# First layer norm by tile and halves, and loads reordered, at the start of a two-block transformer kernel

## The chip, the cores and the metric

The kernel runs on one core of a Trainium2 chip. The metric is device time in microseconds (us) of one execution. The kernel before was run three times.

## What is computed

The reference is a chain of transformer blocks on x of shape 1 x 256 x 1024 in float32: a block with two layers (mixer of latent attention, retention and block attention, then a dense feed-forward in the first and a mixture of experts in the second layer), then a second block with dilated attention, gating and cross attention. Only its first two steps matter here:

```
x = layer_norm(x, ln_emb_g, ln_emb_b)      # 256 rows, each over 1024 columns
h = x @ w_in[0]                            # 1024 -> 2656 columns
```

## The kernel before

The 256 rows of x are two tiles (t = 0, 1) of 128 partitions. Both x and every weight are split into a high part of type float32r (whi, xth) and the rest (wlo, xtl); a product is three matmuls, lines 577 to 579. All weights come as one stream of chunks through six raw buffers, loaded in order by SyncE (`load`, line 399; from the seventh chunk on a load waits for a low part to be done). For each chunk ScalarE makes the high part (`hi`, line 1514, busy line 1518) and VectorE the low part (`lo`, line 2009, busy line 2011); there are three places for split chunks, so the high part of chunk 3 waits until TensorE has released chunk 0. `advance(n)` makes the parts up to chunk n; LEAD is 2. The order of work on each engine is the order of the code; semaphores tie the engines together.

The input projection of a layer has six groups of columns. Group 0 (416 columns) uses chunks 0 and 1 (1664 numbers a partition), group 1 (512 columns) chunks 2 and 3 (2048 numbers a partition). Chunks 4 and 5 (1152 and 768 numbers) are for the latent projections. `in_part(g, j, t)` (line 1121) multiplies the j-th chunk of group g with tile t: 12 matmuls. If the stage is not in BY_TILE, group 0 runs chunk 0 for both tiles, then chunk 1 for both; if it is, tile 0 with both chunks, then tile 1, and the turns of tile 1 (`turn_half`) stand inside these parts.

The start, before the first mixer:
- SyncE loads both tiles of x, the scale row (rows0, into bc), the identity, the shift row (rows1), then chunks 0 to 5 (lines 404 to 420).
- GpSimd issues the columns (cols), then waits for the first normed tile and issues the constant table (cst, 2180 KB), the positions and, when both tiles are normed, the next two rows.
- VectorE waits for both tiles of x, takes mean and variance of tile 0 (`measure_first`, line 2078) and norms the two tiles in whole rows of 1024 (`norm_embedding`, line 2104; busy lines 2114 to 2119).
- ScalarE takes the second moments of tile 1 (`ln_roots`, line 1549).
- TensorE turns both tiles by 128 x 128 (`transpose_x`, line 606, busy line 611) into four banks, and ScalarE and VectorE copy and split them in four pieces (`split_x`, lines 1542 and 2032).
- Around that the engines make chunks 0 (before the split) and 1 (behind it). VectorE then waits for cols and the constant table (lines 2655 and 2656) before it goes on to chunk 2.

The helpers by tile are there already and are used by the later norms ln1_0, ln2_0 and ln1_1: `norm_by_halves` (line 2051), `split_half` (line 2044), `split_tile` (line 1560), `turn_half` (line 652), `ln_by_tile` (line 1583, whose second moments are lines 1592 to 1595).

Of the kernel before, what the change touches and what calls it, by code (L numbers as in the profile page):

```python
# [17 lines left out]
ALU = mybir.AluOpType  # L18
ACT = mybir.ActivationFunctionType
# [6 lines left out]
T = 2  # L26
S = T * P
D = 1024
# [4 lines left out]
LEAD = SPLIT - 1  # L33
# [55 lines left out]
B_TQ, B_S, B_TP, B_O = 7, 0, 1, 2  # L89


BY_TILE = ("ln1_0", "ln2_0", "ln1_1")
X_TURNS = ((2, 3), (6, 7))


# [71 lines left out]
def _by_layer(*parts, skip=()):  # L167
    return [(f"{n}{l}", c) for l in LAYERS for n, c in parts if f"{n}{l}" not in skip]
# [17 lines left out]
    "x": [("emb", T)] + _by_layer(("lat", T), ("mix", 5), ("ln1_", T), ("ln2_", T))  # L186
    + [("mix2", 2 * T)],

    "half": _by_layer(("ln1_", T), ("ln2_", T), skip=("ln2_1",)),

    "mv": [("emb", 1)] + _by_layer(("ln1_", 1), ("ln2_", 1), skip=("ln2_1",)) + [("ln2_1", T)],

# [63 lines left out]
def program(nc, stream, x_in, mem_in, pos_in, consts, route_in, cols_in, rows_in, ws_in, blank_in, out):  # L256
    with ExitStack() as ctx:
# [5 lines left out]
        def sem(name):  # L263
            if name not in sems:
                sems[name] = ctx.enter_context(nc.semaphore(name))
            return sems[name]

        def at(stage, kind, count):

            if stage == "f1" and kind in UNIT_KINDS:  # L270
                return sem(f"f1_{kind}"), count
            return sem(kind), count + before(stage, kind)
# [21 lines left out]
        x = sb("resid", [P, T, D])  # L294
        r = sb("r", [P, T, D])
# [101 lines left out]
        @block.sync  # L397
        def _(sp):
            def load(c):
                if not (isinstance(c.n, int) and c.n < RAW):  # L400
                    sp.wait_ge(lo_done, c.n - RAW + 1)
                sp.dma_start(raw[:, c.raw, 0:c.width], stream[c.n, :, 0:c.width]).then_inc(landed[c.raw], 16)

            for t in range(T):
                sp.dma_start(r[:, t, :], x_in[t * P:(t + 1) * P, :]).then_inc(sem(f"x_in{t}"), 16)
            sp.dma_start(bc[:, 0, :], rows_in[0, :].partition_broadcast(P)).then_inc(sem("rows0"), 16)
            sp.dma_start(ident, consts[:, CONST_AT["ident"][0]:CONST_AT["ident"][1]]).then_inc(sem("ident_in"), 16)
            sp.dma_start(bc[:, 1, :], rows_in[1, :].partition_broadcast(P)).then_inc(sem("rows1"), 16)
            n = 0
            while n < NCHUNK:  # L410
                if any(n == AT[f] for f in ("f0", "f1", "f2", "f3")):
                    name = next(f for f in ("f0", "f1", "f2", "f3") if n == AT[f])
                    loops = 3 * (U_MOE if name == "f1" else U_FF) // LB
                    with sp.Fori(0, loops) as it:
                        for j in range(LB):
                            load(Chunk(n + j, it))
                    n += loops * LB
                else:
                    load(Chunk(n))
                    n += 1  # L420
            for t in range(T):
                sp.wait_ge(sem("final"), t + 1)
                sp.dma_start(out[t * P:(t + 1) * P, :], r[:, t, :]).then_inc(sem("stored"), 16)
            sp.wait_ge(sem("stored"), 16 * T)
# [3 lines left out]
        def _(pool):  # L428
# [6 lines left out]
                    sem(f"rows{n}"), 16)  # L435

            pool.dma_start(cols[:, :], cols_in).then_inc(sem("cols_in"), 16)
            pool.wait_ge(*at("emb", "x", 1))
            pool.dma_start(cst[:, 0:CONST_AT["ident"][0]], consts[:, 0:CONST_AT["ident"][0]]).then_inc(sem("const_in"), 16)
            pool.dma_start(posi[:, :], pos_in).then_inc(sem("pos_in"), 16)  # L440
            chained = [0]
# [132 lines left out]
        def _(pe):  # L574
# [31 lines left out]
            def transpose_x(stage, src, kn=KD, banks=(0, 1, 2, 3), ready=None):  # L606

                for t in range(T):
                    pe.wait_ge(*(ready(t) if ready else at(stage, "x", t + 1)))
                    for k in range(kn):  # L610
                        m = pe.transpose(ps[banks[k // 2]][:, (k % 2) * S + t * P:(k % 2) * S + (t + 1) * P],
                                         src[:, t, k * P:(k + 1) * P], ident)
                        if t == T - 1 and (k % 2 == 1 or k == kn - 1):
                            m.then_inc(sem("tr"), 1)
# [727 lines left out]
                        m.then_inc(used if (l, t, n) == (0, 1, 1) else sem("pj"), 1)  # L1342

            pe.wait_ge(sem("ident_in"), 16)
            transpose_x("emb", x)
            xt_stage = "emb"
            for l in range(DEPTH):
                mixer(l, xt_stage)
# [155 lines left out]
        def _(act):  # L1504
# [3 lines left out]
            def link(ins):  # L1508

                chained[0] += 1  # L1510
                ins.then_inc(sem("act_chain"), 1)
                act.wait_ge(sem("act_chain"), chained[0])
# [7 lines left out]
            def advance(upto):  # L1520

                while cursor[0] <= min(upto, NCHUNK - 1):
                    hi(Chunk(cursor[0]))
                    cursor[0] += 1
# [21 lines left out]
                        act.activation(dst[:, k, :], ps[banks[b]][:, (k % 2) * S:(k % 2 + 1) * S], ACT.Copy,  # L1546
                                       scale=cols[:, gain + k:gain + k + 1]).then_inc(sem("xh"), 1)

            def ln_roots(stage, ready):


                act.wait_ge(*ready)
                link(act.activation(x[:, 1, :], r[:, 1, :], ACT.Copy, accum_out=ss[:, 0:1]))
                link(act.activation(ss[:, 1:2], ss[:, 0:1], ACT.Copy, scale=-1.0 / D))
                act.wait_ge(*at(stage, "mv", 1))
                act.activation(sd[:, 0:1], mv[:, 0, 1:2], ACT.Sqrt, bias=eps[:, 0:1]).then_inc(sem("sd"), 1)
                link(act.activation(x[:, 1, :], r[:, 1, :], ACT.Square, bias=ss[:, 1:2], accum_out=ss[:, 2:3]))
                act.activation(sd[:, 1:2], ss[:, 2:3], ACT.Sqrt, bias=eps[:, 0:1], scale=1.0 / D).then_inc(sem("sd"), 1)

            def split_tile(stage, t):  # L1560

                for b in range(2):
# [4 lines left out]
            def last_norm():  # L1567
# [3 lines left out]
                for t in range(T):  # L1571
# [4 lines left out]
                    for k in range(KD):  # L1576
                        act.wait_ge(*at("n1", "tr", 4 * t + k % 4 + 1))
                        if k >= 4:
                            act.wait_ge(*at("n1", "xt", KD * t + k - 3))
                        act.activation(xth[:, k, t * P:(t + 1) * P],  # L1580
                                       ps[TURN_BANKS[k % 4]][:, (k // 4) * S + t * P:(k // 4) * S + (t + 1) * P], ACT.Copy, scale=cols[:, COLS["ffn1"] + k:COLS["ffn1"] + k + 1]).then_inc(sem("xh"), 1)

            def ln_by_tile(stage, ready, upto=0):


                act.activation(sd[:, 3:4], eps[:, 0:1], ACT.Sqrt)
                act.wait_ge(*at(stage, "mv", 1))
                act.activation(sd[:, 0:1], mv[:, 0, 1:2], ACT.Sqrt, bias=eps[:, 0:1]).then_inc(sem("sd"), 1)
                advance(upto)
                split_tile(stage, 0)  # L1590
                act.wait_ge(*ready)
                link(act.activation(x[:, 1, :], r[:, 1, :], ACT.Copy, accum_out=ss[:, 0:1]))
                link(act.activation(ss[:, 1:2], ss[:, 0:1], ACT.Copy, scale=-1.0 / D))
                link(act.activation(x[:, 1, :], r[:, 1, :], ACT.Square, bias=ss[:, 1:2], accum_out=ss[:, 2:3]))
                act.activation(sd[:, 1:2], ss[:, 2:3], ACT.Sqrt, bias=eps[:, 0:1], scale=1.0 / D).then_inc(sem("sd"), 1)
                split_tile(stage, 1)

            def rms_roots(stage, tile_ready, junk, src):
# [273 lines left out]

            act.wait_ge(sem("eps_set"), 2)
            act.activation(sd[:, 3:4], eps[:, 0:1], ACT.Sqrt)
            ln_roots("emb", (sem("x_in1"), 16))
            advance(0)
            split_x("emb")
            advance(LEAD - 1)
            act.wait_ge(sem("cols_in"), 16)
            for l in range(DEPTH):  # L1880
                mixer(l)
# [117 lines left out]
        def _(dve):  # L1999
# [3 lines left out]
            def link(ins):  # L2003

                chained[0] += 1
                ins.then_inc(sem("dve_chain"), 1)
                dve.wait_ge(sem("dve_chain"), chained[0])
# [6 lines left out]
            def advance(upto):  # L2014

                while cursor[0] <= min(upto, NCHUNK - 1):
                    lo(Chunk(cursor[0]))
                    cursor[0] += 1
# [84 lines left out]

            def norm_embedding():

                for t in range(T):
                    dve.wait_ge(sem(f"x_in{t}"), 16)
                measure_first("emb", lambda n: None)
                dve.wait_ge(sem("rows0"), 16)
                for t in range(T):  # L2110
                    mean, sign = (mv[:, 0, 0:1], ALU.subtract) if t == 0 else (ss[:, 1:2], ALU.add)
                    if t == 1:
                        dve.wait_ge(*at("emb", "sd", T))
                    link(dve.scalar_tensor_tensor(out=r[:, t, :], in0=r[:, t, :], scalar=mean, in1=bc[:, 0, :],
                                                  op0=sign, op1=ALU.mult))
                    dve.wait_ge(*at("emb", "sd", t + 1))
                    link(dve.reciprocal(rstd[:, t:t + 1], sd[:, t:t + 1]))
                    dve.wait_ge(sem("rows1"), 16)
                    dve.scalar_tensor_tensor(out=x[:, t, :], in0=r[:, t, :], scalar=rstd[:, t:t + 1], in1=bc[:, 1, :],
                                             op0=ALU.mult, op1=ALU.add).then_inc(sem("x"), 1)  # L2120

            def half_sum(stage, t, n):

# [525 lines left out]
            for slot in range(2):  # L2649
                dve.memset(lone_keys[slot][HD * (1 - slot):HD * (2 - slot)], 0.0).then_inc(sem("blank_keys"), 1)  # L2650
            norm_embedding()
            advance(0)
            split_x("emb")
            advance(LEAD - 1)
            dve.wait_ge(sem("cols_in"), 16)
            dve.wait_ge(sem("const_in"), 16)
            for l in range(DEPTH):
# [374 lines left out]
```

## Time and profile before

| | us |
|---|---|
| median of 3 runs | 2038.57 |
| lowest and highest | 2038.34, 2038.59 |
| the profiled execution | 2039.05 |
| its span, first to last instruction | 2037.2 |

The page of the profile gives the busy time of each engine (PE is TensorE, PEld its weight loads, DVE VectorE, ACT ScalarE, POOL GpSimd, SP SyncE), the chain of work that ended last and the costliest groups of instructions. DVE is busy for 74% of the span, ACT for 61%. The timeline lists instructions in order of time: start, duration, engine, line, operation, output <- input, count, and in brackets the idle time of the engine before it and what ended it. Some rows merge several like instructions. Times count from the start of the span.

### The profile page before, as it was taken

The page shows a single profiled execution, that of the slowest core. Times are in us where ns is not written, and L with a number is a line of the kernel's source. Part 1 is how long each engine was busy: PE and PEld are TensorE (multiplying, and loading weights), DVE is VectorE, ACT ScalarE, POOL GpSimd, SP SyncE. Part 2 cuts the span into 40 slices and gives each one's busy share as a digit, 9 for nine tenths or more (in the row PEclk, how much of TensorE's full clock was granted, in tenths as well). Part 3 has the DMA queues.
Part 4 walks back from the last instruction along what each step waited for, and adds up shares of the span by engine and source line. Part 5 has one row for each costly group of instructions (what it writes and reads, how often), then busy time and mean ns, then how long its engine had stood idle before and what let it go on. Part 6 is the DMA issues. An engine that isn't in the chain of part 4 may idle for free.

```text
span 2037.2 us, 26427 instructions
## 1 busy us (share of the span) xinstructions
PE 1993.5 (98%) x9638; PEld 1668.3 (82%) x9638; DVE 1512.2 (74%) x1543; ACT 1244.7 (61%) x1324; POOL 103.6 (5%) x102
## 2 busy tenths in 40 slices
PE   7999999999999999999999999999899999999998
PEld 6978887889888888888888888887688889798886
DVE  6675546676988998898999889899864456655554
ACT  5555444555777777777777777776644455444443
POOL 0011000001000000000000000023000003000000
PEclk9999999999999999999999999999999999999999
DMA  8347654344999999999999999999755554444550
GB/s 330 121 149 293 220 186 154 137 181 174 420 385 383 378 377 369 389 374 381 378 380 384 378 381 377 367 399 372 279 216 185 185 176 165 145 146 176 187 190 33
DMA packets 79658, 555.06 MB, mean 272 GB/s; under 512 B 8976, under 2 KB 9104, under 8 KB 17632
## 3 DMA queue, kind: packets, MB, share of 16 engines
q1 hardware_dynamic: 73728, 522.98, 67.7%
q0 software_dynamic: 5840, 30.85, 4.0%
q8 instruction: 61, 1.00, 0.2%
q14 instruction: 29, 0.24, 0.0%
HBM read 544.88 MB, written 12.58 MB: 274 GB/s over the span
## 4 chain that ended last, share of the span: by engine, by line
PE 92%; DVE 5%; ACT 1%; issue 1%; DMA 0%; POOL 0%; SPq 0%; DVEq 0%; ACTq 0%
PE ps L577 29%; PE ps L579 28%; PE ps L578 28%; DVE wlo L2011 2%; PE ps L895 1%; PE ps L788 1%; ACT whi L1518 1%; PE ps L1217 0%; PE ps L1193 0%; PE ps L1224 0%; PE ps L1093 0%; PE ps L1073 0%; DMA bc<-in_rows 0%; PE ps L1241 0%; PE ps L1240 0%
## 5 line engine op out<-in xcount | busy, mean ns | idle before, releaser
L2011 DVE TENSOR_TENSOR wlo<-raw,whi 128x2048 fp32r<-128x2048 f32 (+4 forms) x505 | 1145.2, 2271 | 288.6 <-ACT whi L1518 282.1
L1518 ACT ACTIVATE whi<-raw 128x2048 fp32r<-128x2048 f32 (+4 forms) x505 | 950.3, 1883 | 182.8 <-PE ps L579 173.6
L577 PE MATMUL ps<-whi,xth 128*128 128x512 f32 (+3 forms) x1856 | 737.5, 397 | 9.0 <-DVE wlo L2011 5.1
L579 PE MATMUL ps<-whi,xtl 128*128 128x512 f32 (+3 forms) x1856 | 716.4, 386 | 0.0
L578 PE MATMUL ps<-wlo,xth 128*128 128x512 f32 (+3 forms) x1856 | 714.7, 385 | 0.0
L577 PEld LDWEIGHTS ps<-whi,xth 128*128 128x128 f32 x1856 | 350.8, 189 | 77.0 <-DVE wlo L2011 9.9
L579 PEld LDWEIGHTS ps<-whi,xtl 128*128 128x128 f32 x1856 | 350.2, 189 | 69.0
L578 PEld LDWEIGHTS ps<-wlo,xth 128*128 128x128 f32 x1856 | 351.5, 189 | 61.6
L579 PE MATMUL ps<-whi,htl 128*128 128x512 f32 (+2 forms) x748 | 290.1, 388 | 0.0
L577 PE MATMUL ps<-whi,hth 128*128 128x512 f32 (+2 forms) x736 | 287.3, 390 | 2.0 <-DVE htl L2304 1.0
L578 PE MATMUL ps<-wlo,hth 128*128 128x512 f32 (+2 forms) x736 | 284.5, 387 | 0.0
L577 PEld LDWEIGHTS ps<-whi,hth 128*128 128x128 f32 x736 | 138.2, 188 | 31.7 <-issue 2.9
L579 PEld LDWEIGHTS ps<-whi,htl 128*128 128x128 f32 x748 | 140.4, 188 | 28.9
L578 PEld LDWEIGHTS ps<-wlo,hth 128*128 128x128 f32 x736 | 138.2, 188 | 26.9
L1680 ACT ACTIVATE prob<-ps 128x256 f32<-128x256 f32 x112 | 43.0, 384 | 90.0 <-PE ps L579 90.0
L1689 ACT ACTIVATE hth<-ps 128x256 fp32r<-128x256 f32 x112 | 43.1, 384 | 83.2 <-PE ps L895 83.2
L1640 ACT ACTIVATE hth<-ps 128x512 fp32r<-128x512 f32 x30 | 17.9, 598 | 90.9 <-PE ps L788 90.9
L1629 ACT ACTIVATE prob<-ps,rstd 128x256 f32<-128x256 f32 x44 | 18.4, 470 | 73.6 <-PE ps L579 73.6
L2186 DVE TENSOR_TENSOR htl<-ps,hth 128x512 fp32r<-128x512 f32 x30 | 20.7, 691 | 43.3 <-ACT hth L1640 43.3
L2172 DVE SCALAR_TENSOR_TENSOR probt<-prob,rstd,ps 128x256 f32<-128x256 f32 x44 | 19.2, 476 | 39.5 <-ACT prob L1629 39.5
L2304 DVE TENSOR_TENSOR htl<-ps,hth 128x256 fp32r<-128x256 f32 x112 | 46.7, 417 | 1.5 <-ACT hth L1689 1.5
L2288 DVE TENSOR_TENSOR probt<-prob,ps 128x256 f32<-128x256 f32 x112 | 46.3, 413 | 0.0
(394 smaller groups left out, 1294.1 us busy)
## 6 DMA issues: line engine op xcount, KB each, us to landing
raw<-in_stream SPq DMA_DIRECT2D x475, 1024.0 KB, 6.6
raw<-in_stream SPq DMA_DIRECT2D x16, 768.0 KB, 4.5
bc<-in_rows POOLq DMA_DIRECT2D x4, 1024.0 KB, 5.8
slot_rows<-in_blank POOLq DMA_DIRECT2D x7, 512.0 KB, 10.6
kc<-slot_rows POOLq DMA_DIRECT2D x7, 512.0 KB, 8.1
sum_rows<-r POOLq DMA_DIRECT2D x7, 512.0 KB, 5.9
raw<-in_stream SPq DMA_DIRECT2D x4, 832.0 KB, 6.4
raw<-in_stream SPq DMA_DIRECT2D x4, 640.0 KB, 3.8
```

Of the source, the lines that this page charges most:

```text
L577: pe.matmul(o, ah, bh, start=start, stop=False, skip_group_check=True)
L578: pe.matmul(o, ah, bl, start=False, stop=False, skip_group_check=True)
L579: return pe.matmul(o, al, bh, start=False, stop=stop, skip_group_check=True)
L788: m = pe.transpose(ps[2][:, k * S + t * P:k * S + (t + 1) * P], hs[:, t, k * P:(k + 1) * P], ident)
L895: m = pe.transpose(ps[1][:, k * P:(k + 1) * P], hs[:, 0, k * P:(k + 1) * P], ident)
L1518: act.activation(whi[:, c.split, 0:c.width], raw[:, c.raw, 0:c.width], ACT.Copy).then_inc(hi_done, 1)
L1680: act.activation(sg[:, 0, :], ps[0][:, 0:FU], ACT.Silu).then_inc(sem("e_sg"), 1)
L1689: act.activation(hth[:, 0:2, 0:P], ps[1][:, 0:2 * P].rearrange("p (k s) -> p k s", k=2), ACT.Copy).then_inc(sem("e_hh"), 1)
L2011: dve.tensor_tensor(wlo[:, c.split, 0:c.width], raw[:, c.raw, 0:c.width], f32(whi[:, c.split, 0:c.width]), ALU.subtract).then_inc(lo_done, 1)
L2186: dve.tensor_tensor(htl[:, 0:2, :], ps[2][:, :].rearrange("p (k s) -> p k s", k=2), f32(hth[:, 0:2, :]), ALU.subtract).then_inc(unit_sem(n ...
L2288: dve.tensor_tensor(hs[:, 0, :], sg[:, 0, :], ps[0][:, FU:2 * FU], ALU.mult).then_inc(sem("e_h"), 1)
L2304: dve.tensor_tensor(htl[:, 0:2, 0:P], ps[1][:, 0:2 * P].rearrange("p (k s) -> p k s", k=2), f32(hth[:, 0:2, 0:P]), ALU.subtract).then_inc( ...
```

## The change

The first norm becomes one of the stages by tile. The loads are issued in another order: tile 0 of x, rows0, identity, rows1, chunk 0, tile 1 of x, chunk 1 and so on. VectorE norms and splits in halves of the columns, with chunk 0 ahead of tile 0's splits and chunk 1 ahead of the norm of tile 1. ScalarE takes the second moments of tile 1 behind chunk 1. GpSimd issues the constant table when both halves of tile 0 are split (semaphore xt at 2), where it waited for the first normed tile. Group 0 of the first input projection runs tile 0 with both chunks, then tile 1. RAISED counts what each semaphore is raised by in each stage.

```
-BY_TILE = ("ln1_0", "ln2_0", "ln1_1")
+BY_TILE = ("emb", "ln1_0", "ln2_0", "ln1_1")
...
-    "half": _by_layer(("ln1_", T), ("ln2_", T), skip=("ln2_1",)),
+    "half": [("emb", T)] + _by_layer(("ln1_", T), ("ln2_", T), skip=("ln2_1",)),
...
-            for t in range(T):
+            def rows_of_x(t):
                 sp.dma_start(r[:, t, :], x_in[t * P:(t + 1) * P, :]).then_inc(sem(f"x_in{t}"), 16)
+
+            rows_of_x(0)
...
+                if n == 1:
+                    rows_of_x(1)
...
-            pool.wait_ge(*at("emb", "x", 1))
+            pool.wait_ge(*at("emb", "xt", 2))
             pool.dma_start(cst[:, 0:CONST_AT["ident"][0]], consts[:, 0:CONST_AT["ident"][0]]).then_inc(sem("const_in"), 16)
...
             pe.wait_ge(sem("ident_in"), 16)
-            transpose_x("emb", x)
...
+            def second_moments(stage, ready):
+
+                act.wait_ge(*ready)
+                link(act.activation(x[:, 1, :], r[:, 1, :], ACT.Copy, accum_out=ss[:, 0:1]))
+                link(act.activation(ss[:, 1:2], ss[:, 0:1], ACT.Copy, scale=-1.0 / D))
+                link(act.activation(x[:, 1, :], r[:, 1, :], ACT.Square, bias=ss[:, 1:2], accum_out=ss[:, 2:3]))
+                act.activation(sd[:, 1:2], ss[:, 2:3], ACT.Sqrt, bias=eps[:, 0:1], scale=1.0 / D).then_inc(sem("sd"), 1)
...
-            ln_roots("emb", (sem("x_in1"), 16))
+            act.wait_ge(*at("emb", "mv", 1))
+            act.activation(sd[:, 0:1], mv[:, 0, 1:2], ACT.Sqrt, bias=eps[:, 0:1]).then_inc(sem("sd"), 1)
             advance(0)
-            split_x("emb")
+            split_tile("emb", 0)
             advance(LEAD - 1)
+            second_moments("emb", (sem("x_in1"), 16))
+            split_tile("emb", 1)
...
             def norm_embedding():
 
-                for t in range(T):
-                    dve.wait_ge(sem(f"x_in{t}"), 16)
+                dve.wait_ge(sem("x_in0"), 16)
                 measure_first("emb", lambda n: None)
                 dve.wait_ge(sem("rows0"), 16)
...
+                dve.wait_ge(sem("rows1"), 16)
+                norm_by_halves("emb", 0, mv[:, 0, 0:1], ALU.subtract)
+                advance(0)
+                for b in range(2):
+                    split_half("emb", 0, b)
+                advance(LEAD - 1)
+                dve.wait_ge(sem("x_in1"), 16)
+                dve.wait_ge(*at("emb", "sd", T))
+                norm_by_halves("emb", 1, ss[:, 1:2], ALU.add)
+                for b in range(2):
+                    split_half("emb", 1, b)
...
             norm_embedding()
-            advance(0)
-            split_x("emb")
-            advance(LEAD - 1)
             dve.wait_ge(sem("cols_in"), 16)
             dve.wait_ge(sem("const_in"), 16)
```

## Rows read from the trace of the kernel before

**Rows 1.** The page: busy time of TensorE, and the chain that ended last.
```profile
PE 1993.5 (98%) x9638; PEld 1668.3 (82%) x9638; DVE 1512.2 (74%) x1543; ACT 1244.7 (61%) x1324; POOL 103.6 (5%) x102
...
PE 92%; DVE 5%; ACT 1%; issue 1%; DMA 0%; POOL 0%; SPq 0%; DVEq 0%; ACTq 0%
```

**Rows 2.** The timeline of all engines, 0 to 28.3 us.
```profile
0.74 0.87 SPq L405 DMA_DIRECT2D r<-in_x  x2
...
5.59 1.28 DVE L2082 BATCH_NORM_STATS2 bn<-r 128x6 f32<-128x512 f32 x2 [4.08 <-DMA r<-in_x]
...
11.43 0.54 POOL L439 DMA_DIRECT2D cst<-in_consts  x1 [9.35 <-DVE resid L2119]
...
11.72 1.59 ACT L1518 ACTIVATE whi<-raw 128x1664 fp32r<-128x1664 f32 x1 [2.75 <-DMA raw<-in_stream]
...
15.55 2.48 DVE L2032 TENSOR_TENSOR xtl<-ps,xth 128x512 fp32r<-128x512 f32 x4
...
16.38 0.69 PE L577 MATMUL ps<-whi,xth 128*128 128x416 f32 x1 [0.52 <-DVE xtl L2032]
...
16.54 3.41 ACT L1518 ACTIVATE whi<-raw 128x1664 fp32r<-128x1664 f32 x2
...
22.41 0.36 PE L579 MATMUL ps<-whi,xtl 128*128 128x416 f32 x1
...
23.75 4.67 DVE L2011 TENSOR_TENSOR wlo<-raw,whi 128x2048 fp32r<-128x2048 f32 x2 [3.68 <-DMA cst<-in_consts]
...
28.28 0.39 PE L577 MATMUL ps<-whi,xth 128*128 128x512 f32 x1
```

**Rows 3.** Issues and time to landing: tile 0, rows1, chunk 0, chunk 1, constants.
```profile
r<-in_x SPq DMA_DIRECT2D x1, 512.0 KB, 3.5
...
bc<-in_rows SPq DMA_DIRECT2D x1, 512.0 KB, 7.0
...
raw<-in_stream SPq DMA_DIRECT2D x1, 832.0 KB, 8.4
...
DMA to landing us min/median/max: 10.0/10.0/10.0
...
cst<-in_consts POOLq DMA_DIRECT2D x1, 2180.0 KB, 12.2
```

**Rows 4.** Queues in 14 to 15, 19 to 20, 22 to 23 us: packets, MB, share.
```profile
q1 hardware_dynamic: 60, 0.43, 103.0%
...
q0 software_dynamic: 17, 0.30, 69.8%
q1 hardware_dynamic: 17, 0.14, 33.0%
...
q0 software_dynamic: 40, 0.12, 31.0%
```

**Rows 5.** The timeline of a later norm by halves, 138 to 147 us.
```profile
138.50 0.75 DVE L2055 SCALAR_TENSOR_TENSOR r<-r,mv,bc 128x512 f32<-128x512 f32 x1
...
140.81 0.75 DVE L2061 SCALAR_TENSOR_TENSOR resid<-r,rstd,bc 128x512 f32<-128x512 f32 x1
...
141.49 0.69 DVE L2048 TENSOR_TENSOR xtl<-ps,xth 128x512 fp32r<-128x512 f32 x1
...
143.53 1.06 ACT L1592 ACTIVATE resid<-r 128x1024 f32<-128x1024 f32 x1 [0.62 <-DVE r L2125]
...
146.23 0.29 ACT L1595 ACTIVATE sd<-ss,eps 128x1 f32<-128x1 f32 x1
```

**Rows 6.** TensorE's idle before two matmuls, and clock of a stretch (after POOL's busy).
```profile
146.48 0.50 PE L577 MATMUL ps<-whi,xth 128*128 128x512 f32 x1 [1.15 <-DVE wlo L2011]
...
1461.93 1.15 PE L665 MATMUL ps<-cst,resid 128*128 128x128 f32 x8 [3.82 <-DVE resid L2216]
...
1459.00:1475.00 16.00, 12.49 (x55) 10.06 (x56) 14.00 (x28) 8.79 (x23) 0.62 (x1) 0.89 0.35 119
```

More of the change, by code:

```diff
@@ L1547, in split_x @@
                                        scale=cols[:, gain + k:gain + k + 1]).then_inc(sem("xh"), 1)
[L1549 to L1558, printed above, removed]
             def split_tile(stage, t):
@@ L1590, in ln_by_tile @@
                 split_tile(stage, 0)
[L1591 to L1595, printed above, removed]
+                second_moments(stage, ready)
                 split_tile(stage, 1)
@@ L2104, in norm_embedding @@
             def norm_embedding():
-                for t in range(T):
-                    dve.wait_ge(sem(f"x_in{t}"), 16)
+                dve.wait_ge(sem("x_in0"), 16)
                 measure_first("emb", lambda n: None)
                 dve.wait_ge(sem("rows0"), 16)
[L2110 to L2120, printed above, removed]
+                dve.wait_ge(sem("rows1"), 16)
[9 more added lines that the diff above has]
+                    split_half("emb", 1, b)
             def half_sum(stage, t, n):
```

## Prediction

> **What bounds the kernel now.** I read the page first. TensorE is busy 1993.5 of 2037.2 us, and the chain that ended last lies 92% on it [rows 1]. So a change at the start can only shift the whole run: what counts is when TensorE starts, and whether it then runs on. Next I read the timeline of the first 30 us [rows 2]. The reader is to see four points. The first projection matmul starts at 16.38 us, released by the last step of splitting the turned activations (DVE line 2032 from 15.55). Group 0 of the input projection (48 matmuls) then runs without a gap. Group 1 starts at 28.28 us, the landmark of my sum. Its first weight chunk, chunk 2, was ready well ahead: its low part was made from 23.75 us, in 2.3 us, so at about 26.0 us. The slack is 2.2 us. That low part did not start earlier because VectorE waits for the constant table (cst), although ScalarE had made the high part by 20.0 us [rows 2]. After 28.28 us the waits of TensorE up to 150 us are all on work that itself follows TensorE (the 1.15 us before 146.48 is the longest, [rows 6]), so I carry a shift of the start of group 1 one to one to the end.
>
> **Landings.** Tile 0 of x is issued at 0.74 us and lands 3.5 later, at 4.24; tile 1 lands at about 5.5, since VectorE, which waits for both, starts at 5.59 [rows 2, 3]. One tile of x costs the queue 1.25 us. The second row (rows1) lands at 2.61 + 7.0 = 9.6, chunk 0 at 3.26 + 8.4 = 11.7, chunk 1 at 3.8 + 10.0 = 13.8 [rows 3]. Tile 1 of x now goes behind chunk 0, so rows1 lands at 8.35 and chunk 0 at 10.45. Chunk 1 has the same bytes ahead of it as before: 13.8.
>
> **Tile 0 to the first matmul.** Statistics of tile 0 start at 4.3 instead of 5.59 and end at about 5.8; that gain is hidden, since the norm now waits for rows1, until 8.45. From the same helper at 138.50: start of the norm to its last half 140.81 + 0.75, so 3.06 us, with the first half out after 1.6 [rows 5]. Here the halves are out at 10.1 and 11.55, and TensorE turns them by 12.7. ScalarE makes the high part of chunk 0 from 10.5 to 12.1 (1.59, [rows 2]), then the high parts of the halves of tile 0 (0.60 each) until 13.3. VectorE makes the low part of chunk 0 from 12.2 to 14.0 and then two half splits of 0.69 us [rows 5], done at 14.7 and 15.3. The first matmul follows at 14.85: 1.5 us earlier than 16.38. Both the shorter queue (1.25) and the half splits (four pieces of 0.6 before, the first of which was enough for the first matmul) are in it.
>
> **Group 0.** Its first 17 matmuls took from 16.38 to 22.41, 0.35 us each, which for 416 columns is the 1.2 GHz level; the other 31 took until 28.28, 0.19 each, the 2.4 GHz level [rows 2]; what TensorE had done before the rise was turns from 11.27 and matmuls from 16.38. The granted clock of the trace reads 1.00 all through this start, so I go by spacing. With the start 1.5 us earlier I expect the rise somewhere from 18.8 to 22.2 us. Tile 0, first chunk: 12 x 0.345 = 4.1, until 19.0. Chunk 1 is ready: high part 13.9 to 15.5, low part until 17.4.
>
> Tile 1 is now inside. ScalarE starts its second moments only behind chunk 1, at 15.5; the same block took from 143.53 to 146.23 + 0.29, 3.0 us [rows 5], so the root is there at 18.5. VectorE waits for it, and behind that wait stand the norm and splits of tile 1 and the low part of chunk 2. The halves of tile 1 come at 20.2 and 21.6. VectorE can split the first half only behind the second norm half: 21.6 to 22.3 at the earliest. TensorE gets there from 20.1 (rise at 18.8) and waits twice, some 0.6 and 0.5 us; with the rise at 22.2 it waits hardly at all, but runs slowly. The second half is turned at 24.1 to 25.2 and its high part is made by 24.75 to 25.9. Group 0 ends at 27.85 to 28.95. The eight turns of tile 1, now within the group, are in this (0.11 to 0.23 us each). So the 1.5 us gained at the start have shrunk to 0.4 us or to a loss of 0.7.
>
> **Chunk 2, which group 1 needs.** Two things now push it back.
> First, ScalarE's order. Its high part used to follow chunk 1 directly (16.54, two pieces, [rows 2]). Now the second moments and both splits of tile 1 stand ahead of it: it runs from 24.75 to 26.65 (25.9 to 27.8 with the late rise). The low part takes 2.28 more: 28.95 at the earliest.
> Second, the constants. GpSimd issued them at 11.43, 0.3 us behind the first x tile, and they landed 12.2 us later, at 23.6, just ahead of the low part at 23.75 [rows 2, 3]. The new condition is the second half split of tile 0, at 15.3: issue at 15.6. Queued behind that wait on GpSimd are the position load and the next rows, both needed late. How long they take: q0 moved nothing of them until 15.0, 3.6 us after the issue; then it got 0.30 MB a us against 0.14 MB of the weight queue, both with 17 packets [rows 4], so the queues take turns by packet and the 17 KB rows of the constants win over the 8 KB rows of weights. Their 2.23 MB ended soon after 22.0 [rows 4], 7.2 us, and landed 1.4 us later. In the new place they start 3.6 us after 15.6, at 19.2, when the weight queue at 0.43 MB a us is in chunk 5, with some 0.25 MB left in rows of 3 KB. Beside those the constants get 17 of 20 parts, 0.37 MB a us, for 4 us, then 0.30 for their last 0.75 MB: 6.5 us, and 1.4 to the landing: 27.1. Bounds: 25.8 if nothing else moves, 27.8 if it takes 12.2 again. I take 27.1, since the packet turns are seen directly. The low part of chunk 2 then runs from 27.2 to 29.5.
>
> *A rule against a row.* The row gives 12.2 us from issue to landing for 2180 KB [rows 3]. The Trainium skill, DMA: Bandwidth & Descriptors, section Anatomy of one DMA, gives about 2.0 us plus the bytes at 436 GB/s, an estimate of 7.1 us here. By that the constants would land at 22.7, the ScalarE order alone would set chunk 2, and the sum below would be +0.7. The trace does not agree, since the transfer shares its engines; I use the row.
>
> **Sum.** Group 1 starts at 29.5 instead of 28.28: +1.2 us. TensorE waits some 1.6 us ahead of it. What comes next has slack: chunk 3, whose high part waits until chunk 0's place is free (the third part of group 0 instead of the second) and follows at 28.5, is ready at 31.8 and needed at 35.0; the latent norm was in time by 3.3 us before and moves by about 0.5. Nothing of the arithmetic is added or removed; splitting the norm of two tiles in halves costs VectorE 0.5 us, all under other work. The profiled execution took 2039.05 us (span 2037.2), 0.48 above the median of 2038.57. So 2040.25 for a profiled run, and 2038.57 + 1.2 = 2039.8 for the median.
>
> **Rivals.**
> *A, chunk 2 is late (forecast): 0.70.* +0.7 (constants early, ScalarE sets it) to +1.9 (constants at 27.8, or late rise): 2039.3 to 2040.5. For it: both causes stand by themselves in the order of the code.
> *B, chunk 2 is in time: 0.16.* Then group 0's end decides: -0.4 us, 2038.2; if tile 1 also never waits, the whole 1.5 passes, 2037.1. For it: the slack was 2.2 us, and landings near the start may be faster than I place them. Against: ScalarE would have to reach chunk 2 two us earlier.
> *C, the wait drops the clock: 0.14.* TensorE idle for 1.6 us could fall back to 1.2 GHz. Behind the 3.82 us wait at 1461.93 the granted clock of the stretch is 0.89 [rows 6]; behind the 1.15 us wait at 146.48 the first matmul took 0.50 and nothing slow followed. My wait is nearer to the second. Price: a slow stretch like 16.38 to 22.2, half of which is lost, some 2.7 us: 2042.5 with +1.2, and 2043.1 with the constants at 27.8. Only the latter is slower by over 0.2%; it decides from a constants' landing of about 27.5 on.
> That the change doesn't do what it says is no rival of its own: the order is written out in the code.
>
> **Numbers.** 2039.8. The range 2038.1 to 2041.3 holds A with some margin and most of B; outside are the full gain and most of C. A measurement of this kernel tells from no change about 0.2%, 4.1 us; nearly all cases lie within. Faster needs group 1 at 24.2 us, which 48 matmuls from 14.85 don't allow unless all run at 2.4 GHz: 0.01. Slower is the end of C, with a little for a later wait that I don't see: 0.05. Same: 0.94.
>
> **What would show it.** First matmul near 14.85; group 1 near 29.5, waiting for the low part of chunk 2 (line 2011); its high part after the splits of tile 1 on ScalarE, from 24.7 on; constants issued near 15.6 and landed near 27. I am wrong if group 1 starts before 28.3, if TensorE never waits on line 2011 near 28 us, or if matmuls of 512 columns, now 0.23 us apart, follow that wait at about twice the spacing.

## The result: slower by 0.13%, with the loss ahead of group 1

The changed kernel takes 2042.53 us (median of 22 runs, 2040.24 to 2045.46), the kernel before, run beside it, 2039.52 (22 runs, 2036.84 to 2042.19). The ratio is 1.0013, interval 1.0007 to 1.0019: by the ratio 2.7 us slower, between 1.4 and 3.9 (the medians stand 3.0 apart). Forecast was 1.2 us slower and 2039.8 us, range up to 2041.3. The three runs known before the change (2038.34 to 2038.59) did not show that the kernel before itself scatters over 5 us. The profiled execution took 2043.17 us, its span is 2041.4, 4.2 more than the span before.

The page of the changed kernel, busy times and the chain that ended last; the lines answer to [rows 1]:

```profile
PE 1991.0 (98%) x9638; PEld 1665.2 (82%) x9638; DVE 1513.7 (74%) x1547; ACT 1246.3 (61%) x1324; POOL 103.3 (5%) x102
...
PE 92%; DVE 5%; ACT 1%; DMA 1%; issue 1%; SPq 0%; POOL 0%; DVEq 0%; ACTq 0%
PE ps L581 28%; PE ps L583 28%; PE ps L582 28%; DVE wlo L2010 2%; PE ps L899 1%; ACT whi L1521 1%; PE ps L792 1%; DMA cst<-in_consts 1%; DMA raw<-in_stream 0%; PE ps L1197 0%; PE ps L1221 0%; PE ps L1228 0%; PE ps L1097 0%; PE ps L1077 0%; PE ps L1244 0%
```

The work is the same, but the constants' load now lies on the chain (DMA 1%, where it was 0%). The timeline of the changed kernel at the start, against [rows 2] (lines 1521, 2010 and 2047 are the high part, the low part and the half split; 581 to 583 are the three matmuls):

```profile
9.76 0.75 DVE L2054 SCALAR_TENSOR_TENSOR r<-r,mv,bc 128x512 f32<-128x512 f32 x1 [4.15 <-DMA bc<-in_rows]
...
11.78 1.59 ACT L1521 ACTIVATE whi<-raw 128x1664 fp32r<-128x1664 f32 x1 [5.84 <-DMA raw<-in_stream]
...
13.41 1.89 DVE L2010 TENSOR_TENSOR wlo<-raw,whi 128x1664 fp32r<-128x1664 f32 x1 [0.58 <-ACT whi L1521]
...
15.22 1.28 DVE L2047 TENSOR_TENSOR xtl<-ps,xth 128x512 fp32r<-128x512 f32 x2
...
16.05 0.69 PE L581 MATMUL ps<-whi,xth 128*128 128x416 f32 x1 [2.05 <-DVE xtl L2047]
...
16.81 0.55 POOL L443 DMA_DIRECT2D cst<-in_consts  x1 [14.72 <-DVE xtl L2047]
...
25.91 3.71 ACT L1521 ACTIVATE whi<-raw 128x2048 fp32r<-128x2048 f32 x2
...
26.05 0.69 DVE L2047 TENSOR_TENSOR xtl<-ps,xth 128x512 fp32r<-128x512 f32 x1 [2.56 <-ACT xth L1556]
...
29.08 4.50 DVE L2010 TENSOR_TENSOR wlo<-raw,whi 128x2048 fp32r<-128x2048 f32 x2 [2.34 <-DMA cst<-in_consts]
...
31.43 0.50 PE L581 MATMUL ps<-whi,xth 128*128 128x512 f32 x1 [2.10 <-DVE wlo L2010]
```

The first matmul starts at 16.05 instead of 16.38, but group 1 at 31.43 instead of 28.28: 3.15 us later, behind a wait of 2.10 us for the low part of chunk 2. VectorE was free for that part from 26.7 on and ScalarE had finished its half at 27.8; it waited for the constants until 29.08. Their issue and landing, with those of rows1 and chunk 0 (columns as in [rows 3]):

```profile
bc<-in_rows SPq DMA_DIRECT2D x1, 512.0 KB, 7.5
...
raw<-in_stream SPq DMA_DIRECT2D x1, 832.0 KB, 9.2
...
DMA to landing us min/median/max: 12.2/12.2/12.2
```

The last line is that of the constants alone (line 443). They took 12.2 us as before, but from 16.81.

### The profile page after: what moved, and what is told of

Its sections match the earlier page's. It is cut to its first block, busy times and chain, and to the rows that moved or that the text cites. A ratio compares the mean times of both kernels' runs of the same rounds, so it can differ in the third digit from the quotient of the medians.

```text
span 2041.4 us, 26426 instructions
## 1 busy us (share of the span) xinstructions
PE 1991.0 (98%) x9638; PEld 1665.2 (82%) x9638; DVE 1513.7 (74%) x1547; ACT 1246.3 (61%) x1324; POOL 103.3 (5%) x102
## 4 chain that ended last, share of the span: by engine, by line
PE 92%; DVE 5%; ACT 1%; DMA 1%; issue 1%; SPq 0%; POOL 0%; DVEq 0%; ACTq 0%
PE ps L581 28%; PE ps L583 28%; PE ps L582 28%; DVE wlo L2010 2%; PE ps L899 1%; ACT whi L1521 1%; PE ps L792 1%; DMA cst<-in_consts 1%; DMA raw<-in_stream 0%; PE ps L1197 0%; PE ps L1221 0%; PE ps L1228 0%; PE ps L1097 0%; PE ps L1077 0%; PE ps L1244 0%
## 5 line engine op out<-in xcount | busy, mean ns | idle before, releaser
L899 PEld LDWEIGHTS ps<-cst,probt 128*128 128x128 f32 x224 | 30.9, 139 | 20.3 <-DVE probt L2286 6.0
```

The source lines that it names most:

```text
L899: m = pe.transpose(ps[1][:, k * P:(k + 1) * P], hs[:, 0, k * P:(k + 1) * P], ident)
```

## The experiments

Two starting points were used: the changed kernel and the kernel before. The number to watch is the start of group 1, read from each timeline. "Ratio" is always to the kernel before, run beside it.

**Second and third profiles.** Unchanged kernels, four profiles.

> The kernel before, unchanged, for a second profile of its start. If the landings scatter from run to run by up to 1.5 us, the scale row lands between 8.2 and 9.1 and group 1 starts between 28.3 and 29.2. If they don't, both are as in the first profile within 0.2 us.

> The changed kernel, unchanged, for a second profile of its start. If its late rows (9.7 us) were one draw, the shift row lands near 8.4, the first matmul is near 14.8, the constants are issued near 15.5 and land near 27.6, and group 1 starts near 30.1. If it is how the new order always comes out, group 1 is again near 31.4.

> The kernel before, a third profile. Group 1 at 28.3 to 28.7, no wait for chunk 2. If the fall of the clock between 108 and 118 us, seen in both profiles so far, belongs to this order of work, it is there again; if it comes by chance, it may be missing.

> The changed kernel, a third profile. Group 1 at 30.5 to 31.5, behind a wait of about 2 us for chunk 2. Waits of 2.10 and 2.12 us left the clock up in the two profiles so far, while waits of 2.18, 2.95 and 4.20 us in other versions were followed by a stretch at 1.2 GHz. If that is by chance, it can follow here too, at some 1.6 us.

| kernel | chunk 0 landed, about | first matmul | constants issued | group 1 | span |
|---|---|---|---|---|---|
| before | 11.7 | 16.38 | 11.43 | 28.28 | 2037.2 |
| before, second | 12.6 | 17.31 | 12.35 | 28.64 | 2039.4 |
| before, third | 11.4 | 16.10 | 11.15 | 27.64 | 2038.2 |
| changed | 11.8 | 16.05 | 16.81 | 31.43 | 2041.4 |
| changed, second | 11.0 | 15.24 | 16.00 | 30.58 | 2040.5 |
| changed, third | 12.0 | 16.27 | 17.04 | 31.48 | 2042.5 |

The landings scatter, by 1.2 us among the three profiles of the kernel before and by 1.0 among those of the changed one, so the late rows of the first profile were partly a draw. The profiles come from several batches on different chips, and it can't be told how much of this is the chip; e7 and e8 below, which have the same loads up to there and ran in one batch, still differ by 0.7. What doesn't scatter much is the distance from the first matmul to group 1: 11.9, 11.3 and 11.5 us before, 15.4, 15.3 and 15.2 after. On the means, the first matmul comes 0.7 us earlier and group 1 3.0 us later (28.19 to 31.16). Between the two lie 1.7 us more for group 0, which now holds the turns and splits of tile 1 (13.3 us from its first matmul to its end, against 11.6), and 2.0 us of waiting for chunk 2: -0.7 + 1.7 + 2.0 = 3.0. The spans differ by 3.2 us on the means. The timed difference, 2.7, is the same within its interval. The third profile of the kernel before misses its expectation (27.64 against 28.3 to 28.7): the scatter is wider than two profiles had shown. The fall of the clock behind the 2 us wait, which was thought possible there, did not come in the third profile of the changed kernel either.

**e1: the constants early.** Changed kernel with

```diff
-            pool.wait_ge(*at("emb", "xt", 2))
+            pool.wait_ge(*at("emb", "x", 1))
```

> The changed kernel, but the constant table is issued when tile 0 is normed (about 13.1 us) and not when it is split (16.8). In the changed kernel group 1 starts at 31.43 us, waiting for the low part of chunk 2, for which the constants (landed 29.0) came last; its high part was done at 27.8. Theory (two causes, the constants first and ScalarE's order 1.2 us behind them): the constants land near 25.3, the low part runs from 27.9 to 30.15, group 1 starts at 30.2, and the time falls by 1.2 us against the changed kernel, still 1.9 above the kernel before. Rival (the constants alone): group 1 starts where group 0 ends, at 29.15, a fall of 2.3 us. Rival (load order alone): no fall.

**e2: ScalarE's half of chunk 2 early.** Changed kernel with

```diff
             second_moments("emb", (sem("x_in1"), 16))
+            advance(LEAD)
             split_tile("emb", 1)
```

> The changed kernel, but ScalarE makes the high part of chunk 2 ahead of the splits of tile 1 (in its idle time from 19.7 to 22.2 us) and not behind them. Theory (the constants come last): the high part is done by 21.6, and nothing else moves: group 1 at 31.4 us, time as the changed kernel within 0.3 us. Rival (ScalarE's order is what sets chunk 2): the low part starts at 26.8, group 1 at 29.15, a fall of 2.3 us.

**e3: both edits.**

> Both edits: constants issued when tile 0 is normed, and the high part of chunk 2 ahead of the splits of tile 1. Theory: chunk 2 is then bound by VectorE alone, low part from 26.8 to 29.05, group 1 at 29.15 us where group 0 ends: 2.3 us below the changed kernel, 0.9 above the kernel before. Rival (something else than chunk 2 holds group 1): it starts later than 29.5.

The low part of chunk 2 and the start of group 1, from the timelines of e1, e2 and e3 (two lines each, in this order):

```profile
27.20 4.49 DVE L2010 TENSOR_TENSOR wlo<-raw,whi 128x2048 fp32r<-128x2048 f32 x2 [1.21 <-ACT whi L1521]
...
29.55 0.50 PE L581 MATMUL ps<-whi,xth 128*128 128x512 f32 x1 [0.96 <-DVE wlo L2010]
```

```profile
26.58 4.49 DVE L2011 TENSOR_TENSOR wlo<-raw,whi 128x2048 fp32r<-128x2048 f32 x2 [0.72 <-DMA cst<-in_consts]
...
28.93 0.50 PE L581 MATMUL ps<-whi,xth 128*128 128x512 f32 x1 [0.48 <-DVE wlo L2011]
```

```profile
25.72 4.48 DVE L2011 TENSOR_TENSOR wlo<-raw,whi 128x2048 fp32r<-128x2048 f32 x2
...
28.23 0.40 PE L581 MATMUL ps<-whi,xth 128*128 128x512 f32 x1
```

The brackets name the cause, whatever the landings were. With early constants the low part waits 1.21 us for ScalarE; with early ScalarE it waits 0.72 for the constants; with both it waits for nothing and TensorE doesn't either. So both causes are real, the constants the later of the two. In all three the first matmul came at 14.5 to 14.9, and from there to group 1 it is 14.7, 14.4 and 13.4 us against 15.3 of the changed kernel. e2's 14.4 is smaller than the theory wanted (15.3, no fall), since its constants took only 11.2 us to land. e1's 14.7 is larger than it wanted (14.1), since group 0 itself took 13.8 us there: 16 of its matmuls ran at the 1.2 GHz level, against 12 to 14 in the changed kernel. The times say less: ratios 1.0016 (1.0007 to 1.0025), 1.0015 (1.0006 to 1.0024) and 1.0010 (1.0001 to 1.0019). They don't show what one edit alone is worth. They do show a gain of both together: e3 ran beside e1 and e2, and on the means of 11 runs each it is 1.4 and 1.8 us faster (95% intervals 0.3 to 2.5 and 0.6 to 3.0).

**e4: chunk 2 ahead of the wait for the constants.** Changed kernel with the edit of e2 and, on VectorE,

```diff
-                for b in range(2):
-                    split_half("emb", 1, b)
+                split_half("emb", 1, 0)
+                advance(LEAD)
+                split_half("emb", 1, 1)
```

> The changed kernel, but both parts of chunk 2 are made ahead of the wait for the constants: the high part between ScalarE's second moments and its splits of tile 1, the low part between the two half splits of tile 1 on VectorE. The constants stay late. Theory (chunk 2's readiness is all that holds group 1): TensorE doesn't wait at the start of group 1; it starts where group 0 ends, some 13.3 us behind the first matmul, so at about 28 us with the rows landed at 8.4 and 29.2 with the late landing of the changed kernel's profile. Rival (the constants matter elsewhere too, as for the latent norm): a wait turns up before 45 us.

```profile
22.54 2.28 DVE L2011 TENSOR_TENSOR wlo<-raw,whi 128x2048 fp32r<-128x2048 f32 x1
...
28.15 2.29 DVE L2011 TENSOR_TENSOR wlo<-raw,whi 128x2048 fp32r<-128x2048 f32 x1 [2.28 <-DMA cst<-in_consts]
...
28.30 0.39 PE L581 MATMUL ps<-whi,xth 128*128 128x512 f32 x1
```

Chunk 2's low part fits into VectorE's idle time inside tile 1, the constants still come at 28.1, now in front of chunk 3, and TensorE has no wait for it (its only waits from 20 to 45 us are two of 0.3 us for half splits). Ratio 1.0004 (0.9995 to 1.0013): no difference to the kernel before can be told any more. By the mean distance of each to the kernel before, e4 is 1.7 us faster than the changed kernel (0.5 to 2.8), so the readiness of chunk 2 made most of the loss of 2.7. The repair ends level and not ahead: the wait is gone, but group 0 by tile still takes 13.7 us here against 11.6 before, which uses up what the earlier first matmul (14.60) gains.

**e5: late constants alone.** Kernel before with

```diff
-            pool.wait_ge(*at("emb", "x", 1))
+            pool.wait_ge(*at("emb", "xt", 1))
```

> The kernel before with one edit: the constant table is issued when the first piece of x is split (about 16.4 us) and not when tile 0 is normed (11.4). Theory (a late constant table is enough by itself): it lands near 28.6, the low part of chunk 2 is made from 28.7 to 31.0, group 1 starts at 31.0 instead of 28.28: 2.7 us above the kernel before, nearly the whole loss of the changed kernel. Rival (the order by tile and the loads make the loss): less than 1 us above the kernel before.

```profile
30.28 4.49 DVE L2011 TENSOR_TENSOR wlo<-raw,whi 128x2048 fp32r<-128x2048 f32 x2 [9.40 <-DMA cst<-in_consts]
...
32.62 0.80 PE L577 MATMUL ps<-whi,xth 128*128 128x512 f32 x1 [4.20 <-DVE wlo L2011]
...
34.07 0.63 PE L577 MATMUL ps<-whi,xth 128*128 128x512 f32 x1
...
38.92 0.40 PE L577 MATMUL ps<-whi,xth 128*128 128x512 f32 x1
```

One moved wait on GpSimd, with nothing else changed, costs 6.1 us: ratio 1.0030 (1.0018 to 1.0043). It is more than the 2.7 expected, for two reasons in the rows. Group 1 starts at 32.62, 4.4 us behind the mean of the kernel before (first matmul 17.18, constants issued 17.35, 12.8 us to landing). And TensorE, idle for 4.20 us, goes on at 0.43 us a matmul instead of 0.23, the 1.2 GHz level, until about 38.5: some 2.8 us more on the way to the next norm. The granted clock of 28 to 38 us reads 0.69. That is rival C of the prediction, in another kernel.

**e6: the old order of loads.** Changed kernel, both tiles of x first.

> The changed kernel with the old order of loads (both tiles of x first). Theory (one tile of x costs the queue 1.25 us): the shift row lands near 9.6 and chunk 0 near 11.7, the first matmul is near 16.0 instead of the 14.8 seen in three of the four profiles with the new order, the constants are issued near 16.8, and group 1 starts near 31.2. Rival (the order of loads is worth nothing, the landings only scatter): first matmul at 14.5 to 15.

Chunk 0's high part starts at 11.60, the first matmul is at 15.87, group 1 at 31.48 behind a wait of 2.95 us, after which the clock falls (granted 0.83 from 28 to 38 us); ratio 1.0026 (1.0016 to 1.0036). In the seven profiles that keep the new order and the old rows, chunk 0's high part starts at 10.2 to 12.0, at 10.9 on the mean; in the five with the old order at 11.4 to 12.6, 12.0 on the mean. The order of loads is worth about 1.1 us there, against the 1.25 that the prediction took for one tile of x, but a single profile can't show it: the three of the kernel before and the three of the changed kernel differ by 0.3 only.

**e7, e8, e9, e10: the queue at the start.** e7 is the changed kernel with the two rows laid out 128 times in main memory. e8 adds the edits of e4. e9 adds to e8 the identity behind chunk 0 and the columns behind the constants. e10 is the kernel before with wide rows, the identity behind rows1 and the columns behind the constants. The line of e7's edit for the scale row (the shift row's load changes likewise; the new input is left out here):

```diff
-            sp.dma_start(bc[:, 0, :], rows_in[0, :].partition_broadcast(P)).then_inc(sem("rows0"), 16)
+            sp.dma_start(bc[:, 0, :], wide_in[0]).then_inc(sem("rows0"), 16)
```

> The changed kernel, but the scale and shift rows stand 128 times in main memory, laid out so ahead, and are loaded as plain 128 x 1024 blocks. Theory (the slow stretch of the queue, 0.22 to 0.36 MB a us instead of 0.43 between 4 and 9 us, comes from 128 reads of one row): the rate stays near 0.43, the shift row lands near 7.4 us, chunk 0 near 9.5, the first matmul near 13.8. Rival (the slow stretch comes from the small packets of the columns and the identity): landings as in the changed kernel, 8.2 to 9.7.

> Both of the last edits: chunk 2 made ahead of the constants, and the rows wide in main memory. Theory: first matmul near 13.8, group 1 near 27.0, 1.3 us ahead of the kernel before, so a time 1 to 1.5 us below it. Rival: no gain over the kernel before, since later falls of the clock set the time.

> The kernel with wide rows and chunk 2 made ahead of the constants, and besides the small-packet loads moved back: the identity behind chunk 0, the columns behind the constants. Theory (the rest of the slow stretch at 5 us, 0.21 to 0.24 MB a us with 102 to 112 packets under 2 KB, is the identity and the columns): the rate stays at 0.37 or more, the shift row lands near 7.5, the first matmul is near 13.8, group 1 near 26.8. Rival (the stretch is slow whatever stands in it): as without the move, 14.3 and 27.3. Time: 1 us below the kernel before by the theory, if the start of group 1 is all that counts.

> The kernel before with the loads alone improved: wide rows, the identity behind the shift row, the columns behind the constants. Theory: the scale row lands near 7.0 instead of 8.2 to 9.1, the first matmul near 15.3, group 1 near 27.2, time 1 us below the kernel before. Rival (VectorE's whole-row norm is the longer path, so the landings don't matter): first matmul within 0.3 us of 16.4.

What the DMA engines moved in one us: 5 to 6 us of e7, then 5 to 6 and 8 to 9 us of e9, then 5 to 6 and 7 to 8 us of the kernel before and 5 to 6 us of e10.

```profile
DMA packets 145, 0.21 MB, mean 213 GB/s; under 512 B 24, under 2 KB 102, under 8 KB 145
```

```profile
DMA packets 86, 0.34 MB, mean 344 GB/s; under 512 B 2, under 2 KB 2, under 8 KB 86
...
DMA packets 184, 0.30 MB, mean 302 GB/s; under 512 B 27, under 2 KB 140, under 8 KB 184
```

```profile
DMA packets 70, 0.23 MB, mean 226 GB/s; under 512 B 14, under 2 KB 14, under 8 KB 70
...
DMA packets 218, 0.39 MB, mean 385 GB/s; under 512 B 26, under 2 KB 138, under 8 KB 218
...
DMA packets 92, 0.36 MB, mean 360 GB/s; under 512 B 4, under 2 KB 4, under 8 KB 92
```

In e7 and e9 the slow microsecond goes where the small packets of the identity go. Wide rows brought the scale row from 6.3 to 5.6 us and left that microsecond in place. But the kernel before is slow (0.23 MB) in a microsecond with hardly a small packet, which wide rows bring to 0.36 (e10), and moves 0.39 MB beside 138 of them. So each theory had a part: the scale row, read 128 times, cost the queue time, and small packets did in some microseconds and not in others; what decides that stayed open. About the 7.4 us expected of e7 for the shift row (found 8.7) came only with the small loads away (e9: issued 1.7, 5.8 later). First matmul 14.99, 14.32 and 13.78 in e7, e8 and e9, where 13.8 was expected of all three; group 1 at 30.28, 27.34 and 27.20 (27.0 and 26.8 expected of e8 and e9). Yet the ratios are 1.0009 (1.0000 to 1.0018), 1.0004 (0.9995 to 1.0013) and 0.9997 (0.9988 to 1.0006). e9 starts group 1 a full us ahead of the kernel before, and no gain can be told. e10 repeated the mistake under study: ScalarE waits for the columns ahead of chunk 2.

```profile
24.43 3.71 ACT L1518 ACTIVATE whi<-raw 128x2048 fp32r<-128x2048 f32 x2 [6.62 <-DMA cols<-in_cols]
```

Its first matmul is at 16.04, group 1 at 28.83 behind a new wait of 1.75 us, ratio 1.0001 (0.9992 to 1.0010): the expectation of 27.2 failed on a wait that I had moved without asking what is queued behind it. The first matmul missed its 15.3 too. In the five profiles with whole-row norms it comes 8.06 to 8.07 us behind the start of the norm of tile 0, which waits for the scale row, and VectorE is the longer path; here that row landed at 7.9 and not at 7.0.

## Why the prediction was wrong in size

**What bounds the kernel:** the prediction was right that a shift at the start is carried to the end, but on the way it isn't carried one to one. On the means of three profiles, group 1 moved by 3.0 us, the first turn of the next norm by 1.5 (140.07 to 141.59), the first turn of the last of these norms by 3.0 (1462.0 to 1465.0), the span by 3.2. The granted clock explains the dip; 108 to 118 us of before and of the changed kernel, the last three columns being the clock, the share of the DMA engines and GB/s:

```profile
108.00:118.00 10.00, 8.64 (x42) 7.28 (x42) 8.91 (x25) 5.63 (x15) 2.17 (x2) 0.83 0.42 148
```

```profile
108.00:118.00 10.00, 8.64 (x61) 7.72 (x60) 9.72 (x23) 7.48 (x21) 2.17 (x2) 1.00 0.29 106
```

In all three profiles of the kernel before the clock falls there, in none of the changed kernel; from group 1 to the next norm it is 111.9 us with that fall and 110.4 without. It also falls there in e1, e8 and e10 and not in e2 to e7 and e9, so it isn't tied to either order of work. What sets it stayed open. The 1.5 us come back later, up to 1462 us: 1.0 on the means in waits of TensorE among the experts, and 0.5 by a single pause in the third profile of the changed kernel. Its waits from 480 to 1455 us, before and changed (total, times, longest):

```profile
PE ps L577 <- DVE wlo L2011: 1.8, 2, 0.9
PE ps L895 <- DVE probt L2288: 1.6, 1, 1.6
PE ps L577 <- DVE htl L2304: 1.0, 1, 1.0
```

```profile
PE ps L899 <- DVE probt L2286: 4.8, 3, 1.7
PE ps L581 <- DVE htl L2302: 1.0, 1, 1.0
```

4.4 us in each of the three profiles of before, 5.8, 5.5 and 5.0 in those of the changed kernel, 4.3 to 6.0 in the other versions. The pause, where the other five of these profiles have 3.82 us:

```profile
1466.71 1.97 PE L669 MATMUL ps<-cst,resid 128*128 128x128 f32 x8 [5.20 <-issue]
```

Nothing in the profile ended its last 1.4 us. I did not forecast either, and why the sums differ was not settled.

**The first matmul:** forecast 14.85, found 16.05, 15.24 and 16.27. The chain was right: with chunk 0's high part started at 11.78, 10.97 and 12.01, the matmul is 4.26 to 4.27 us behind it each time, and 4.35 was the sum. The first step that failed is the landing of chunk 0, put at 10.45 from a single profile; on the mean its high part started at 11.59. Forecast gain 1.5 us, found 0.7. This makes 1.0 of the 1.66 us by which group 1 came behind the forecast (31.16 against 29.5).

**Group 0:** forecast to end at 27.85 to 28.95, found 29.3 in the first profile, 13.3 us behind the first matmul where the forecast had 13.0 to 14.1. The rise of the clock came at 20.2 us, inside the range. TensorE waited twice for 0.28 us instead of 0.6 and 0.5.

**Chunk 2:** both pushes were right, and their order (e1, e2, e3). ScalarE's high part ran from 25.91, 9.9 us behind the first matmul, exactly as forecast. The constants were issued 0.76 us behind the first matmul, as forecast (0.75). The second step that failed is their landing, a mis-sized term: 11.5 us forecast by the packet turns beside chunks 4 and 5, 12.2, 12.2 and 12.0 measured in the three profiles of the changed kernel. The queues from 21 to 22 us, of the changed kernel and of e2 (columns as in [rows 4]):

```profile
q0 software_dynamic: 16, 0.28, 65.0%
q1 hardware_dynamic: 16, 0.11, 26.4%
...
q0 software_dynamic: 20, 0.35, 81.7%
q1 hardware_dynamic: 23, 0.07, 16.8%
```

In the first profile of the changed kernel the constants' first bytes moved some 3.8 us behind the issue (3.6 forecast), and they landed some 1.3 us behind the last (1.4 forecast). What was too short are the 6.5 us between. The forecast counted on rows of 3 KB beside them and 0.37 MB a us; the weight queue's packets were already of about 7 KB on the mean, the constants got 0.28 to 0.31, and it took some 7.1 us. In e2 the packets beside them were of 3 KB, they got 0.30 to 0.40 from 19 to 25 us, and landed after 11.2 us; e4, with much the same rates, took 12.7. So the turns by packet set the rate, but don't fix the landing: across all the profiles it is 11.2 to 12.8 us with issues from 11.1 to 17.4 us. The 12.2 that I had as the upper bound should have been the value. This term is the other 0.6 us. From a first matmul at 15.85, the mean of the three, 0.76 to the issue, 12.2 to the start of the low part and 2.35 to group 1 give 31.16, which is the mean found.

**Rivals:** B, chunk 2 in time, did not happen in the changed kernel and happened in e3, e4, e8 and e9. C did not happen in it: 2.10, 2.12 and 1.74 us of waiting left the clock up. In other versions it did, behind waits of 2.18 (e7), 2.95 (e6) and 4.20 us (e5), with 0.83, 0.83 and 0.69 as the granted clock of 28 to 38 us. So C was nearer than the chance of 0.14 that I gave it. The rule of the Trainium skill, DMA: Bandwidth & Descriptors, section Anatomy of one DMA, gives an estimate of 7.1 us for the constants. The measured 12.0 to 12.2 decide: the first bytes moved only after some 3.8 us, and the transfer went at about 0.30 MB a us beside the weight queue.

**The range:** it held a shift of up to 2.7 us on top of a median of three runs. The kernel before, run 22 times, moved by 0.95 us itself, and each start scatters by a us. A margin of 0.8 us over the worst case of the forecast did not cover that. The measured 2042.5 is 2.7 us above the forecast 2039.8: 0.95 of it is this baseline, and the rest is the 1.8 us by which the shift was forecast too small (1.2 against 3.0 in the rows).

## What to carry to other kernels

When a load is issued behind a later event, find who waits for it in the code, even if that waiter doesn't use it yet, and what is queued behind that wait: here a table that chunk 2 doesn't need held chunk 2. Put the weight preparation that TensorE needs next ahead of such waits and into idle time of the engines (e4), and shift a load's whole measured time from issue to landing rather than a computed one. For a few us at the start, read several profiles: one profile's landings are a draw.

## What the runs showed of the hardware

Loads issued at the same times land up to 1.8 us apart from one profile to the next (chunk 0 in the new order, 10.2 to 12.0 us), over several chips. While the scale row, one row of 4 KB read 128 times, was on its way (5 to 7 us of the kernel before), the DMA engines moved 0.22 to 0.23 MB a us, and 0.36 to 0.39 in e10, where it comes from 128 rows. Beside the small packets of a 64 KB load in rows of 512 bytes they moved 0.21 MB (e7), 0.30 (e9) or 0.39 (the kernel before) in one us, against 0.43 without. A wait of TensorE of 2.1 to 2.2 us was followed by the 1.2 GHz level in one profile (2.18) and not in two (2.10, 2.12); behind 2.95 and 4.20 us it was, at 1.6 and 2.8 us. Such falls come elsewhere in the kernel too, not at the same places in each execution; the one at 108 to 118 us costs 1.5 us. That they make the scatter of some 5 us between executions is not shown: between 100 and 2000 us the three profiles of the changed kernel have 3, 4 and 2 of them, with spans of 2041.4, 2040.5 and 2042.5 us.
